# Gate tiles of a RG-LRU layer: neighbour rows stacked by ScalarE and VectorE instead of by transfers, for six of ten tiles

## The chip, the cores and the metric

One Trainium2 chip, one of its cores. The metric is the device time of one execution in microseconds (us). TensorE (PE) does the matrix products, ScalarE (ACT) and VectorE (DVE) the elementwise work, GpSimd (POOL) splits weights, SyncE (SP) issues the weight transfers. All arithmetic on the matrix side is fp32 accuracy from fp32r operands: a matrix or an activation is kept as a high part and the rest that the high part leaves (`hi`, `lo`), and a product is three matmuls, hi by hi, hi by lo and lo by hi.

## The reference, cut to what matters

A hybrid residual block on 1024 tokens of width 1024: a combined input projection, a Griffin recurrent branch of width 1280 next to sliding-window attention, a merge, an output projection, then SwiGLU. The change touches the two gates of the recurrent branch only:

```python
u = causal_depthwise_conv(u, conv_w) + conv_b            # width 1280
ub = u.reshape(B, S, 16, 80)                             # 16 blocks of 80 channels
r = sigmoid(einsum("bsnc,ncd->bsnd", ub, w_rg) + b_rg)   # block-diagonal
i = sigmoid(einsum("bsnc,ncd->bsnd", ub, w_ig) + b_ig)
log_a = -8 * r * softplus(-lru_lambda); a = exp(log_a)
b = sqrt(-expm1(2 * log_a)) * (i * u)
h = scan(h[t] = a[t] * h[t-1] + b[t]);  out = h * gelu(lru_gate)
```

The blocks have 80 channels and the tiles of the chip 128, so an output tile of 128 channels needs its own 128 channels of u and, at its edges, some channels of the tile before it or of the tile after it (up to 64).

## The kernel before, in words

The tokens are worked on in two halves of 512 (`h` = 0 and 1), so every matmul here has 512 columns. The 1280 channels are ten tiles, `j` = 0 to 9. For every tile, TensorE first computes the u projection (24 matmuls, `project`), and an iteration `j` of the loop `recurrent` on TensorE is: u projection of tile j, the gates of tile j-2 (`gates`), the gelu branch's projection of tile j (24 matmuls). The gates of tiles 8 and 9 come in `kvq`, each behind a projection of k.

ScalarE, in iteration j and strictly in this order: `conv_in` (copies of the projection and the first tap of tile j), `lru_out_hi` of tile j-3, `gate_fns` of tile j-2 (two tanh out of the gates' banks, exp, tanh; they wait for `gates(j-2)` of TensorE), `conv_hi` (the high part of the convolved tile j, called `uc_hi`, line 1383), `gate_root` (a table load and a square root, L1418), `mix` (DMA issues), `decay` (L1430, which waits for VectorE), `gelu` (L1424). VectorE does the other taps, the low part `uc_lo` (`conv_lo`, L1933, which waits for conv_hi), and the recurrence of tile j-2.

How neighbour rows reach a gate tile: matmuls contract over partitions, so rows of another tile have to lie on partitions of one operand.

- Tiles 1, 2, 3, 6, 7, 8 (`MIXED`) need rows of both neighbours. `mix` issues, once uc_lo of tile j exists, one DMA of 64 partitions (256 KB, both parts) from tile j into the operand `mix_hl` of tile j-1 and one into that of tile j+1, where these are MIXED. `mix_hl` has three slots (tile modulo 3). The gate then takes three matmuls of its own rows and three of the mixed operand, for each of the two gates: six a gate.
- Tiles 4, 5, 9 (`NEAR`) need 32 rows of one neighbour. Three DMAs of 64 KB stack the high part, the low part and the high part again on 96 partitions, and the weights are stacked to match (high, high, low), so one matmul (L927) takes the place of three: four a gate.
- Tile 0 needs rows of tile 1 only and reads tile 1's own operand: six a gate.

`gates` on TensorE waits, before its first matmul, for uc_lo of tile j+1 and for `mix_made`, the count of the DMAs of its slot. It also waits for its weights (`w_lo_made`): SyncE loads them (`load_gates`), GpSimd splits them (`split_gates`), four ring slots deep, a slot of weights being free again when TensorE has finished the block four before it (`blocks_done`).

Of the kernel before, what the change touches and what calls it, by code (L numbers as in the profile page):

```python
# [35 lines left out]
P = 128  # L36
# [33 lines left out]

MIXED = (1, 2, 3, 6, 7, 8)


NEAR = {4: (3, P - 32), 5: (6, 0), 9: (8, P - 32)}
STACK = ((0, 0), (32, 1), (64, 0))
STACKED = 96


def mix_count(h, j):
    same = range(j % 3, KR, 3)
    dmas = [2 if i in MIXED else len(STACK) if i in NEAR else 0 for i in same]
    return 16 * (h * sum(dmas) + sum(dmas[:j // 3 + 1]))

GATED = {"step": 0, "tail": 8}
A_STEP = [2, 2, 2, 2] + [3, 3, 2, 2]
# [100 lines left out]
def build(nc, x_d, par_d, alibi_d, eye_d, w_d, x1_d, out_d):  # L188
    with ExitStack() as ctx:
# [11 lines left out]
        def sem(name):  # L201
            return ctx.enter_context(nc.semaphore(name))
# [154 lines left out]
        def p1_raw(t):  # L357
# [39 lines left out]
        r_made, i_made, th_made, exp_made, root_made, a_made, gelu_made, lru_hi_made = (  # L397
            sem("r_made"), sem("i_made"), sem("th_made"), sem("exp_made"), sem("root_made"),
            sem("a_made"), sem("gelu_made"), sem("lru_hi_made"))
        iu_made, loss_made, amp_made, b_made, scanned, h_kept, lru_made, lru_lo_made = (  # L400
            sem("iu_made"), sem("loss_made"), sem("amp_made"), sem("b_made"), sem("scanned"),
            sem("h_kept"), sem("lru_made"), sem("lru_lo_made"))
# [101 lines left out]
        def a21_there(t):  # L504
            return (up_one_loaded[1], 16) if t == 1 else (up_loaded[1], 16 * single_loads(t))

        block = ctx.enter_context(nc.Block())


        @block.sync  # L510
        def _(sp_eng):
# [9 lines left out]
            def load_gates(dram, g, sizes, n, i0):  # L521

                off, i, half = 0, i0, slice(0, P // 2)
                for b, size in enumerate(sizes):
                    s = b % RING
                    wait_pos(sp_eng, w_lo_made, n + b - RING + 1)
                    if size == 4:
                        sp_eng.dma_start(w_raw[:, s, 0:CAP], dram[g, :, off:off + CAP])\
                            .then_inc(w_loaded[s], 16)
                    elif i in MIXED:  # L530
                        sp_eng.dma_start(w_raw[0:P // 2, s, P:2 * P],
                                         dram[g, 0:P // 2, off + 2 * P:off + 3 * P]).then_inc(mix_loaded[s], 16)
                        sp_eng.dma_start(w_raw[P // 2:P, s, P:2 * P],
                                         dram[g, P // 2:P, off:off + P]).then_inc(mix_loaded[s], 16)
                        sp_eng.dma_start(w_raw[:, s, 0:P], dram[g, :, off + P:off + 2 * P])\
                            .then_inc(w_loaded[s], 16)
                    elif i not in NEAR:
                        sp_eng.dma_start(w_raw[:, s, 0:2 * P], dram[g, :, off:off + 2 * P])\
                            .then_inc(w_loaded[s], 16)
                    else:  # L540
                        own = off + P
                        near, r = off if NEAR[i][0] < i else own + P, NEAR[i][1]
                        sp_eng.dma_start(w_raw[0:STACKED, s, P:2 * P],
                                         dram[g, r:r + 32, near:near + P]
                                         .rearrange("(o r) c -> o r c", o=1)
                                         .broadcast_to([len(STACK), 32, P])).then_inc(mix_loaded[s], 16)
                        sp_eng.dma_start(w_raw[:, s, 0:P], dram[g, :, own:own + P])\
                            .then_inc(w_loaded[s], 16)
                    off += size * P
                    i += size < 4 and sizes[b - 1] < 4  # L550
# [119 lines left out]
        def _(pool):  # L670
# [36 lines left out]
            def split_gates(sizes, n, i0):  # L707
                i = i0
                for b, size in enumerate(sizes):
                    s, w = b % RING, slice(0, (4 if size == 4 else 2) * P)  # L710
                    pool.wait_ge(w_loaded[s], (n // RING + b // RING + 1) * 16)
                    if size < 4 and i:
                        used[s] += 2 if i in MIXED else 1
                        pool.wait_ge(mix_loaded[s], 16 * used[s])
                    pool.wait_ge(blocks_done, n + b - RING + 1)
                    if size == 4 or i not in NEAR:
                        nc.gpsimd.tensor_scalar(w_hi[:, s, w], w_raw[:, s, w], 1.0, 0.0,  # L717
                                                ALU.mult, ALU.add).then_inc(w_hi_made, 1)
                    else:
                        nc.gpsimd.tensor_scalar(w_hi[:, s, 0:P], w_raw[:, s, 0:P], 1.0, 0.0,  # L720
                                                ALU.mult, ALU.add).then_inc(w_stacked, 1)
                        r, near = slice(0, STACKED), slice(P, 2 * P)
                        nc.gpsimd.tensor_scalar(w_hi[r, s, near], w_raw[r, s, near], 1.0, 0.0,
                                                ALU.mult, ALU.add).then_inc(w_hi_made, 1)
                        stacked.append(n)
                    if size < 4:
                        split_gate_lo(n + b, s, i)
                    else:
                        pool.wait_ge(w_hi_made, n + b + 1)
                        nc.gpsimd.tensor_tensor(w_lo[:, s, w], w_raw[:, s, w], rd(w_hi[:, s, w]),  # L730
                                                ALU.subtract).then_inc(w_lo_made, 1)
                    i += size < 4 and sizes[b - 1] < 4
# [111 lines left out]
        def _(pe):  # L844
# [58 lines left out]
            def gates(h, j, n, slot):  # L903

                J = j + KR * h
                pe.wait_ge(uc_lo_made, J + (1 if j == KR - 1 else 2))
                if j == KR - 1:
                    pe.wait_ge(r_made, J)
                    pe.wait_ge(i_made, J)
                if j:  # L910
                    pe.wait_ge(mix_made[j % 3], mix_count(h, j))
                own_hi, own_lo = uc_hi[:, j % 4, :], uc_lo[:, j % 4, :]
                for g in range(2):
                    s, out = (slot + g) % RING, ps[:, 4 + g, :]
                    pe.wait_ge(w_lo_made, n + g + 1)
                    own, near = slice(0, P), slice(P, 2 * P)
                    mm(out, w_hi[:, s, own], own_hi, start=True, stop=False)
                    mm(out, w_hi[:, s, own], own_lo, start=False, stop=False)
                    mm(out, w_lo[:, s, own], own_hi, start=False, stop=False)
                    if j not in NEAR:  # L920
                        near_hi, near_lo = ((mix_hi[:, j % 3, :], mix_lo[:, j % 3, :]) if j else
                                            (uc_hi[:, 1, :], uc_lo[:, 1, :]))
                        mm(out, w_hi[:, s, near], near_hi, start=False, stop=False)
                        mm(out, w_hi[:, s, near], near_lo, start=False, stop=False)
                        last = mm(out, w_lo[:, s, near], near_hi, start=False, stop=True)
                    else:
                        last = mm(out, w_hi[0:STACKED, s, near], mix_hi[0:STACKED, j % 3, :],  # L927
                                  start=False, stop=True)
                    last.then_inc(blocks_done, 1)
# [399 lines left out]
        def _(act):  # L1329
# [51 lines left out]
            def conv_hi(h, j, q):  # L1381
                act.wait_ge(taps, (j + KR * h) * 3 + 3)
                fn(uc_hi[:, q, :], uc_of(q), ACT.Copy).then_inc(uc_hi_made, 1)

            def mix(h, j):

                act.wait_ge(uc_lo_made, j + KR * h + 1)
                for to, r in ((j - 1, slice(0, P // 2)), (j + 1, slice(P // 2, P))):
                    if to in MIXED:
                        act.dma_start(rd(mix_hl[r, :, to % 3, :]), rd(uc_hl[r, :, j % 4, :]))\  # L1390
                            .then_inc(mix_made[to % 3], 16)
                    elif to in NEAR and NEAR[to][0] == j:
                        r = slice(NEAR[to][1], NEAR[to][1] + 32)
                        for row, part in STACK:
                            act.dma_start(rd(mix_hi[row:row + 32, to % 3, :]), rd(uc_hl[r, part, j % 4, :]))\
                                .then_inc(mix_made[to % 3], 16)

            def gate_fns(h, j, n):
                J = j + KR * h
# [477 lines left out]
        def _(dve):  # L1877
# [52 lines left out]
            def conv_lo(h, j, q):  # L1930
                J = j + KR * h
                dve.wait_ge(uc_hi_made, J + 1)
                tt(uc_lo[:, q, :], uc_of(q), rd(uc_hi[:, q, :]), ALU.subtract)\  # L1933
                    .then_inc(uc_lo_made, 1)

            def recurrence(h, j, q):
                J = j + KR * h
# [663 lines left out]
```

## Time and profile before

| | |
|---|---|
| time, median of 3 runs | 1620.09 us (1619.33 to 1626.31) |
| the profiled execution | 1621.06 us, of which the span is 1619.2 |
| granted TensorE clock, mean | 0.997 |
| TensorE busy | 1603.6 us, 99% of the span, 7390 matmuls |
| GpSimd, VectorE, ScalarE busy | 1234.4 (76%), 905.0 (56%), 572.3 us (35%) |
| chain that ended last | TensorE 90% |
| neighbour transfers | 24 of 256 KB (landing 4.7 us after issue, median), 18 of 64 KB (4.3 us) |

The first half's gates run from about 45 to 164 us of the span, the second half's from about 505 to 624 us. In the rows below, a gate tile begins on TensorE with its L917 (own high part); L925 is the last matmul of a MIXED gate. A bracket at the end of a row gives how long the engine had been idle before that instruction and what released it.

### The profile page before, as it was taken

What the parts mean: (1) busy time and instruction counts of PE and PEld (TensorE: products, weight loads), DVE (VectorE), ACT (ScalarE), POOL (GpSimd) and SP (SyncE); (2) the same over time, 40 slices, a digit from 0 to 9 for tenths busy, and PEclk for the clock granted to TensorE, in tenths of its full rate; (3) what the DMA queues carried; (4) which work ended last, traced back from release to release, by engine and by line L of the source; (5) the groups of instructions that cost most, each with busy time, mean ns of one, the idle gap of its engine ahead of it and who ended that gap; (6) DMA issues with size and microseconds to landing.
All of it is one profiled execution on the core that took longest, in us unless ns stands there. A gap on an engine that the chain in (4) does not pass through costs nothing.

```text
span 1619.2 us, 24286 instructions
## 1 busy us (share of the span) xinstructions
PE 1603.6 (99%) x7390; PEld 1327.0 (82%) x7390; DVE 905.0 (56%) x1158; ACT 572.3 (35%) x1078; POOL 1234.4 (76%) x1330
## 2 busy tenths in 40 slices
PE   9999999999999999999999999999999999999997
PEld 7888888888888888888888878888888888788887
DVE  6565646652165666676622579677865558405502
ACT  4787335532226885255422244100010013102100
POOL 5787866777777788777777777788887778877875
PEclk9999999999999999999999999999999999999999
DMA  5445432233344454522333583344422222733632
GB/s 165 131 120 131 132 91 80 74 101 93 97 144 128 121 133 114 166 77 74 92 97 95 150 286 107 97 118 117 119 75 75 65 65 69 245 93 114 222 107 87
DMA packets 121462, 188.86 MB, mean 117 GB/s; under 512 B 13668, under 2 KB 45796, under 8 KB 121380
## 3 DMA queue, kind: packets, MB, share of 16 engines
q1 hardware_dynamic: 97476, 144.03, 32.1%
q10 hardware_dynamic: 23904, 43.79, 8.2%
q8 instruction: 45, 0.74, 0.2%
q14 instruction: 37, 0.30, 0.1%
HBM read 162.73 MB, written 17.56 MB: 111 GB/s over the span
## 4 chain that ended last, share of the span: by engine, by line
PE 90%; DVE 4%; issue 2%; ACT 2%; ACTq 0%; DMA 0%; POOL 0%; DVEq 0%; SPq 0%; POOLq 0%
PE ps L872 14%; PE ps L871 14%; PE ps L870 14%; PE ps L1128 8%; PE ps L1127 8%; PE ps L1129 8%; PE ps L1225 4%; PE ps L1226 4%; PE ps L1227 4%; PE ps L950 1%; PE ps L946 1%; PE ps L947 1%; PE ps L1038 1%; DVE rows L2152 1%; DVE rows_r L2311 1%
## 5 line engine op out<-in xcount | busy, mean ns | idle before, releaser
L688 POOL TENSOR_TENSOR w_lo<-w_raw,w_hi 128x512 fp32r<-128x512 f32 (+2 forms) x374 | 448.3, 1199 | 31.2
L685 POOL TENSOR_SCALAR w_hi<-w_raw 128x512 fp32r<-128x512 f32 (+2 forms) x374 | 242.5, 648 | 194.4 <-PE ps L872 127.3
L872 PE MATMUL ps<-h_hi,w_lo 128*128 128x512 f32 x672 | 263.8, 393 | 0.0
L871 PE MATMUL ps<-h_lo,w_hi 128*128 128x512 f32 x672 | 263.6, 392 | 0.0
L870 PE MATMUL ps<-h_hi,w_hi 128*128 128x512 f32 x672 | 262.1, 390 | 0.7 <-DVE g_h L1950 0.6
L870 PEld LDWEIGHTS ps<-h_hi,w_hi 128*128 128x128 f32 x672 | 126.2, 188 | 28.9 <-DVE g_h L1950 1.5
L871 PEld LDWEIGHTS ps<-h_lo,w_hi 128*128 128x128 f32 x672 | 126.2, 188 | 27.5
L872 PEld LDWEIGHTS ps<-h_hi,w_lo 128*128 128x128 f32 x672 | 126.3, 188 | 26.1
L1127 PE MATMUL ps<-t,w_hi 128*128 128x512 f32 x352 | 138.2, 392 | 0.6 <-POOL w_lo L763 0.5
L1128 PE MATMUL ps<-t,w_hi 128*128 128x512 f32 x352 | 138.7, 394 | 0.0
L1129 PE MATMUL ps<-t,w_lo 128*128 128x512 f32 x352 | 136.6, 388 | 0.0
L1894 DVE TENSOR_TENSOR acc<-acc,sq 128x512 f32<-128x512 f32 x31 | 33.7, 1088 | 146.4 <-ACT sq L1620 134.2
L717 POOL TENSOR_SCALAR w_hi<-w_raw 128x512 fp32r<-128x512 f32 (+1 forms) x100 | 65.3, 653 | 45.5 <-PE ps L872 40.5
L730 POOL TENSOR_TENSOR w_lo<-w_raw,w_hi 128x512 fp32r<-128x512 f32 x72 | 93.8, 1303 | 6.0
L763 POOL TENSOR_TENSOR w_lo<-w_raw,w_hi 128x512 fp32r<-128x512 f32 x60 | 87.0, 1451 | 5.0
L1717 ACT ACTIVATE rstd_a<-rstd_a 128x512 f32<-128x512 f32 x22 | 13.9, 632 | 194.9 <-DVE rstd_a L2298 194.9
L1127 PEld LDWEIGHTS ps<-t,w_hi 128*128 128x128 f32 x352 | 66.1, 188 | 16.8 <-issue 1.4
L1129 PEld LDWEIGHTS ps<-t,w_lo 128*128 128x128 f32 x352 | 66.1, 188 | 14.8
L1128 PEld LDWEIGHTS ps<-t,w_hi 128*128 128x128 f32 x352 | 66.2, 188 | 13.1
L2119 DVE SCALAR_TENSOR_TENSOR tmp<-tmp,ps 128x512 f32<-128x512 f32 x16 | 11.0, 688 | 114.0 <-PE ps L872 114.0
L1620 ACT ACTIVATE sq<-ps 128x512 f32<-128x512 f32 (+1 forms) x15 | 9.0, 598 | 178.8 <-PE ps L1227 174.7
L1539 ACT ACTIVATE prob<-prob,stat 128x128 f32<-128x128 f32 x128 | 49.7, 389 | 63.3 <-DVE stat L2048 63.3
(389 smaller groups left out, 4105.7 us busy)
## 6 DMA issues: line engine op xcount, KB each, us to landing
w_raw<-w_f SPq DMA_DIRECT2D x68, 256.0 KB, 3.2
w_raw<-w_step SPq DMA_DIRECT2D x64, 256.0 KB, 2.8
w_raw<-w_b SPq DMA_DIRECT2D x64, 256.0 KB, 3.1
w_raw<-w_d SPq DMA_DIRECT2D x64, 256.0 KB, 2.7
w_raw<-w_a SPq DMA_DIRECT2D x96, 128.0 KB, 2.1
w_raw<-w_q SPq DMA_DIRECT2D x32, 256.0 KB, 3.1
w_raw<-w_o SPq DMA_DIRECT2D x32, 256.0 KB, 3.1
mix_hl<-uc_hl ACTq DMA_DIRECT2D x24, 256.0 KB, 4.7
```

Source lines behind the costliest of these rows:

```text
L685: nc.gpsimd.tensor_scalar(w_hi[:, s, w], w_raw[:, s, w], 1.0, 0.0, ALU.mult, ALU.add).then_inc(w_hi_made, 1)
L688: nc.gpsimd.tensor_tensor(w_lo[:, s, w], w_raw[:, s, w], rd(w_hi[:, s, w]), ALU.subtract).then_inc(w_lo_made, 1)
L717: nc.gpsimd.tensor_scalar(w_hi[:, s, w], w_raw[:, s, w], 1.0, 0.0, ALU.mult, ALU.add).then_inc(w_hi_made, 1)
L730: nc.gpsimd.tensor_tensor(w_lo[:, s, w], w_raw[:, s, w], rd(w_hi[:, s, w]), ALU.subtract).then_inc(w_lo_made, 1)
L763: nc.gpsimd.tensor_tensor(w_lo[:, s, :], src, rd(w_hi[:, s, :]), ALU.subtract)\
L870: mm(out, w_hi[:, s, w], x_hi, start=(k == 0), stop=False)
L871: mm(out, w_hi[:, s, w], x_lo, start=False, stop=False)
L872: last = mm(out, w_lo[:, s, w], x_hi, start=False, stop=(k == total - 1))
L1127: mm(ps[:, bank, :], w_hi[:, slot, w], x_hi[:, k, :], start=(q == 0), stop=False)
L1128: mm(ps[:, bank, :], w_hi[:, slot, w], x_lo[:, k, :], start=False, stop=False)
L1129: last = mm(ps[:, bank, :], w_lo[:, slot, w], x_hi[:, k, :], start=False, stop=(q == K2 - 1))
L1225: mm(out, w_hi[:, s, w], hi(k), start=(k == 0), stop=False)
```

## The change

Tiles 2 and 7 leave MIXED for a new group `BOTH`, and tile 0 joins NEAR. For these and for 4, 5 and 9 no DMA brings neighbour rows any more. Instead `conv_hi` of ScalarE, right after it has written the high part of tile j, copies 32 rows of it to each operand that needs them (each copy 32 partitions by 512), and `conv_lo` of VectorE, right after the low part, writes 32 rows of that (by the same subtraction):

- a NEAR tile: two copies on ScalarE (partitions 0 to 31 and 64 to 95), one on VectorE (32 to 63). One matmul for the neighbour, as before; tile 0 gets four matmuls a gate in place of six.
- a BOTH tile: from each neighbour 32 rows of the high part on ScalarE and 32 of the low part on VectorE, 128 partitions in all. The weights are loaded twice over to match, and two matmuls (high weights, low weights) take the place of three: five a gate in place of six.

By source tile, ScalarE gets three copies and VectorE two in each of j = 1 (for 2 and 0), 3 (for 2 and 4), 6 (for 7 and 5) and 8 (for 7 and 9), and none for the other j. `mix` is left with the transfers for tiles 1, 3, 6 and 8 (8 a half, of 21). SyncE issues five loads for a BOTH block in place of three, and two for a block of tile 0 in place of one; GpSimd splits a block of tile 0 in four instructions in place of two.

```diff
-MIXED = (1, 2, 3, 6, 7, 8)
-NEAR = {4: (3, P - 32), 5: (6, 0), 9: (8, P - 32)}
+MIXED = (1, 3, 6, 8)
+BOTH = (2, 7)
+NEAR = {0: (1, 0), 4: (3, P - 32), 5: (6, 0), 9: (8, P - 32)}
...
+        def near_of(j):
+            return [(to, slice(r, r + 32)) for to, (of, r) in NEAR.items() if of == j]
+        def both_of(j):
+            return ([(j + 1, slice(P - 32, P), 32)] if j + 1 in BOTH else
+                    [(j - 1, slice(0, 32), 0)] if j - 1 in BOTH else [])
...  # SyncE, load_gates
+                    elif i in BOTH:
+                        for row in range(0, P, 64):
+                            sp_eng.dma_start(w_raw[row:row + 32, s, P:2 * P],
+                                             dram[g, 0:32, off + 2 * P:off + 3 * P]).then_inc(mix_loaded[s], 16)
+                            sp_eng.dma_start(w_raw[row + 32:row + 64, s, P:2 * P],
+                                             dram[g, P - 32:P, off:off + P]).then_inc(mix_loaded[s], 16)
+                        sp_eng.dma_start(w_raw[:, s, 0:P], dram[g, :, off + P:off + 2 * P])\
                             .then_inc(w_loaded[s], 16)
...  # TensorE, gates
-                if j:
+                if j in MIXED:
                     pe.wait_ge(mix_made[j % 3], mix_count(h, j))
+                elif j in BOTH:
+                    pe.wait_ge(both_hi_made, both_count(h, j))
+                    pe.wait_ge(both_lo_made, both_count(h, j))
+                else:
+                    pe.wait_ge(near_hi_made, 2 * near_count(h, j))
+                    pe.wait_ge(near_lo_made, near_count(h, j))
...
+                    if j in BOTH:
+                        mm(out, w_hi[:, s, near], mix_hi[:, j % 3, :], start=False, stop=False)
+                        last = mm(out, w_lo[:, s, near], mix_hi[:, j % 3, :], start=False, stop=True)
...  # ScalarE
             def conv_hi(h, j, q):
                 act.wait_ge(taps, (j + KR * h) * 3 + 3)
                 fn(uc_hi[:, q, :], uc_of(q), ACT.Copy).then_inc(uc_hi_made, 1)
+                for to, r, row in both_of(j):
+                    act.wait_ge(uc_hi_made, j + KR * h + 1)
+                    fn(mix_hi[row:row + 32, to % 3, :], rd(uc_hi[r, q, :]), ACT.Copy)\
+                        .then_inc(both_hi_made, 1)
+                for to, r in near_of(j):
+                    act.wait_ge(uc_hi_made, j + KR * h + 1)
+                    for row in (0, 64):
+                        fn(mix_hi[row:row + 32, to % 3, :], rd(uc_hi[r, q, :]), ACT.Copy)\
+                            .then_inc(near_hi_made, 1)
...  # mix
-                    elif to in NEAR and NEAR[to][0] == j:
-                        r = slice(NEAR[to][1], NEAR[to][1] + 32)
-                        for row, part in STACK:
-                            act.dma_start(rd(mix_hi[row:row + 32, to % 3, :]), rd(uc_hl[r, part, j % 4, :]))\
-                                .then_inc(mix_made[to % 3], 16)
...  # VectorE, conv_lo, behind the subtraction that makes uc_lo
+                for to, r, row in both_of(j):
+                    tt(mix_hi[row + 64:row + 96, to % 3, :], uc_of(q)[r, :], rd(uc_hi[r, q, :]),
+                       ALU.subtract).then_inc(both_lo_made, 1)
+                for to, r in near_of(j):
+                    tt(mix_hi[32:64, to % 3, :], uc_of(q)[r, :], rd(uc_hi[r, q, :]), ALU.subtract)\
+                        .then_inc(near_lo_made, 1)
```

## Rows read from the trace of the kernel before

**Rows 1.** The page, busy us, share of the span, instructions.
```profile
PE 1603.6 (99%) x7390; PEld 1327.0 (82%) x7390; DVE 905.0 (56%) x1158; ACT 572.3 (35%) x1078; POOL 1234.4 (76%) x1330
```

**Rows 2.** The page, chain that ended last, shares of the span by engine.
```profile
PE 90%; DVE 4%; issue 2%; ACT 2%; ACTq 0%; DMA 0%; POOL 0%; DVEq 0%; SPq 0%; POOLq 0%
```

**Rows 3.** Timeline of PE: first matmul of gate tiles 1, 3, 6, 8, and 1 again.
```profile
58.87 0.39 PE L917 MATMUL ps<-uc_hl,w_hi 128*128 128x512 f32 x1
...
86.34 0.39 PE L917 MATMUL ps<-uc_hl,w_hi 128*128 128x512 f32 x1
...
125.97 0.47 PE L917 MATMUL ps<-uc_hl,w_hi 128*128 128x512 f32 x1
...
153.68 0.39 PE L917 MATMUL ps<-uc_hl,w_hi 128*128 128x512 f32 x1
...
518.73 0.39 PE L917 MATMUL ps<-uc_hl,w_hi 128*128 128x512 f32 x1
```

**Rows 4.** Waits, 28 to 182 us: who for whom, us, times, longest.
```profile
POOL w_hi L717 <- PE ps L872: 20.2, 22, 1.5
```

**Rows 5.** DMA issues at 80.98, 120.60, 148.32, 514.20: count, KB, us to landing.
```profile
mix_hl<-uc_hl ACTq DMA_DIRECT2D x1, 256.0 KB, 4.8
...
mix_hl<-uc_hl ACTq DMA_DIRECT2D x1, 256.0 KB, 5.3
...
mix_hl<-uc_hl ACTq DMA_DIRECT2D x1, 256.0 KB, 4.6
...
mix_hl<-uc_hl ACTq DMA_DIRECT2D x1, 256.0 KB, 3.7
```

**Rows 6.** Timeline of ACT, 65 to 82 us: iterations 3 and 4.
```profile
65.92 0.57 ACT L1383 ACTIVATE uc_hl<-ps 128x512 fp32r<-128x512 f32 x1
66.51 1.28 ACT L1418 ACT_TABLE_LOAD   x1
...
69.98 0.64 ACT L1430 ACTIVATE g_a<-g_r 128x512 f32<-128x512 f32 x1 [1.54 <-DVE g_s L1943]
...
72.91 0.20 ACT L1369 ACTIVATE u_raw<-u_carry 128x3 f32<-128x3 f32 x1 [0.39 <-PE ps L872]
...
75.64 0.69 ACT L1403 ACTIVATE g_r<-ps,half_b 128x512 f32<-128x512 f32 x1 [0.58 <-PE ps L925]
...
80.98 0.67 ACTq L1390 DMA_DIRECT2D mix_hl<-uc_hl  x1
```

**Rows 7.** Timeline of ACT, 113 to 121 us: iteration 7.
```profile
113.23 0.20 ACT L1369 ACTIVATE u_raw<-u_carry 128x3 f32<-128x3 f32 x1
...
114.76 0.62 ACT L1435 ACTIVATE lru_hi<-g_h 128x512 fp32r<-128x512 f32 x1
115.29 0.67 ACT L1403 ACTIVATE g_r<-ps,half_b 128x512 f32<-128x512 f32 x1
...
120.60 0.65 ACTq L1390 DMA_DIRECT2D mix_hl<-uc_hl  x1
```

**Rows 8.** Timeline of ACT, 140 to 149 us: iteration 9.
```profile
140.10 0.21 ACT L1369 ACTIVATE u_raw<-u_carry 128x3 f32<-128x3 f32 x1 [0.20 <-PE ps L872]
...
142.98 0.69 ACT L1403 ACTIVATE g_r<-ps,half_b 128x512 f32<-128x512 f32 x1 [0.73 <-PE ps L925]
...
148.32 0.71 ACTq L1390 DMA_DIRECT2D mix_hl<-uc_hl  x1
```

**Rows 9.** Timeline of ACT, 502 to 515 us: second half, iterations 1 and 2.
```profile
502.68 0.60 ACT L1424 ACTIVATE gy<-ps 128x512 f32<-128x512 f32 x1 [1.41 <-PE ps L872]
...
512.85 0.60 ACT L1383 ACTIVATE uc_hl<-ps 128x512 fp32r<-128x512 f32 x1 [0.86 <-DVE ps L1927]
...
514.20 0.60 ACTq L1390 DMA_DIRECT2D mix_hl<-uc_hl  x1
```

**Rows 10.** Timeline of ACT at 613 us: small copies.
```profile
613.16 0.30 ACT L1489 ACTIVATE k_hi<-k_hi 128x128 fp32r<-128x128 f32 x1
613.36 0.41 ACT L1490 ACTIVATE v_hl<-v_hl 64x256 fp32r<-64x256 f32 x1
```

More of the change, by code:

```diff
@@ L69, with both_count, near_count @@
 V_BLOCKS = [4, 4, 4, 4]
-MIXED = (1, 2, 3, 6, 7, 8)
-NEAR = {4: (3, P - 32), 5: (6, 0), 9: (8, P - 32)}
-STACK = ((0, 0), (32, 1), (64, 0))
+MIXED = (1, 3, 6, 8)
+BOTH = (2, 7)
+NEAR = {0: (1, 0), 4: (3, P - 32), 5: (6, 0), 9: (8, P - 32)}
+NEAR_LIST = list(NEAR)
 STACKED = 96
 def mix_count(h, j):
-    same = range(j % 3, KR, 3)
-    dmas = [2 if i in MIXED else len(STACK) if i in NEAR else 0 for i in same]
-    return 16 * (h * sum(dmas) + sum(dmas[:j // 3 + 1]))
+    same = [i for i in MIXED if i % 3 == j % 3]
+    return 32 * (h * len(same) + same.index(j) + 1)
+def both_count(h, j):
+    return 2 * (len(BOTH) * h + BOTH.index(j) + 1)
+def near_count(h, j):
+    return len(NEAR) * h + NEAR_LIST.index(j) + 1
 GATED = {"step": 0, "tail": 8}
@@ L399, in build @@
             sem("a_made"), sem("gelu_made"), sem("lru_hi_made"))
+        near_hi_made, near_lo_made = sem("near_hi_made"), sem("near_lo_made")
+        both_hi_made, both_lo_made = sem("both_hi_made"), sem("both_lo_made")
         iu_made, loss_made, amp_made, b_made, scanned, h_kept, lru_made, lru_lo_made = (
@@ L536, in load_gates @@
                             .then_inc(w_loaded[s], 16)
-                    elif i not in NEAR:
-                        sp_eng.dma_start(w_raw[:, s, 0:2 * P], dram[g, :, off:off + 2 * P])\
+                    elif i in BOTH:
[5 more added lines that the diff above has]
+                        sp_eng.dma_start(w_raw[:, s, 0:P], dram[g, :, off + P:off + 2 * P])\
                             .then_inc(w_loaded[s], 16)
                     else:
-                        own = off + P
+                        own = off + (P if i else 0)
                         near, r = off if NEAR[i][0] < i else own + P, NEAR[i][1]
@@ L545, in load_gates @@
                                          .rearrange("(o r) c -> o r c", o=1)
-                                         .broadcast_to([len(STACK), 32, P])).then_inc(mix_loaded[s], 16)
+                                         .broadcast_to([STACKED // 32, 32, P])).then_inc(mix_loaded[s], 16)
                         sp_eng.dma_start(w_raw[:, s, 0:P], dram[g, :, own:own + P])\
@@ L711, in split_gates @@
                     pool.wait_ge(w_loaded[s], (n // RING + b // RING + 1) * 16)
-                    if size < 4 and i:
-                        used[s] += 2 if i in MIXED else 1
+                    if size < 4:
+                        used[s] += 2 if i in MIXED else 4 if i in BOTH else 1
                         pool.wait_ge(mix_loaded[s], 16 * used[s])
@@ L919, in gates @@
                     mm(out, w_lo[:, s, own], own_hi, start=False, stop=False)
-                    if j not in NEAR:
-                        near_hi, near_lo = ((mix_hi[:, j % 3, :], mix_lo[:, j % 3, :]) if j else
-                                            (uc_hi[:, 1, :], uc_lo[:, 1, :]))
+                    if j in BOTH:
+                        mm(out, w_hi[:, s, near], mix_hi[:, j % 3, :], start=False, stop=False)
+                        last = mm(out, w_lo[:, s, near], mix_hi[:, j % 3, :], start=False, stop=True)
+                    elif j not in NEAR:
+                        near_hi, near_lo = mix_hi[:, j % 3, :], mix_lo[:, j % 3, :]
                         mm(out, w_hi[:, s, near], near_hi, start=False, stop=False)
```

## The prediction

> **What bounds the kernel now.** I read the page first, then the chain, then the timelines of the two stretches in which gates are computed. The page: TensorE is busy for 1603.6 of 1619.2 us [rows 1], and the chain that ended last lies on it for 90% [rows 2]. So a matmul that goes is worth its full pace, and a wait of TensorE costs its full length. The timeline of TensorE gives the pace: from the first matmul of gate tile 1 (58.87) to that of tile 3 (86.34) there are 120 (two gate tiles of 12, four projections of 24), 27.47 / 120 = 0.229 us each [rows 3]. (A row's own 0.39 is longer because matmuls overlap.)
>
> The second thing to see is how near TensorE is to waiting there. Between two gate tiles it has 48 projection matmuls, 11.0 us. In that time a closed chain runs: gates of tile j-2 end, ScalarE computes its four gate functions, then the high part of tile j, VectorE the low part, the transfer to tile j-1 is issued, lands, and TensorE may start the gates of j-1. Issue to landing is 4.8 us for the one issued at 80.98 [rows 5, 6], so it landed at 85.78, 0.56 ahead of the 86.34 at which tile 3 began. For tile 6 it was issued at 120.60 and took 5.3 [rows 5, 7]: 125.90, and tile 6 began at 125.97, its first matmul lasting 0.47 instead of 0.39 [rows 3], the mark of a short stall. For tile 8: 148.32 + 4.6 = 152.92 against 153.68 [rows 3, 5, 8]. So the margins are 0 to 0.8 us, and from landing to start it takes 0.07 (125.90 to 125.97).
>
> **What the change removes from TensorE.** Tile 0 loses two matmuls a gate, tiles 2 and 7 one each: (4 + 2 + 2) a half, 16 in all, 16 x 0.229 = 3.7 us. That is the gain if nothing else moved.
>
> **What it adds on ScalarE.** Three copies of 512 elements a partition behind the high part of tiles 1, 3, 6 and 8, ahead of the table load for the square root. The trace has no copy of 32 partitions by 512. Nearest rows: a copy of 128 x 128 lasts 0.30, one of 64 x 256 0.41 [rows 10]: twice the elements on half the partitions, and longer, so the partitions don't count. The high part itself, 128 x 512, lasts 0.57 [rows 6], and two instructions in a row of this length start 0.53 apart (114.76, 115.29) [rows 7]. Three, with a short wait for ScalarE's own write ahead of the first, make 1.7 us. Bounds: 3 x 0.20 = 0.6 by the shortest activation (128 x 3) and 3 x 0.69 = 2.1 by the longest of the high part's kind (L1403) [rows 6]. I take 1.7, the row nearest in length.
>
> The Trainium skill speaks against the change here: its page "ScalarE: Activation LUTs", section "What ACT_TABLE_LOAD costs", gives an activation with immediates as 186 ns and 0.833 ns for each element along the partition, with 93 ns of overlap between neighbours, so that cutting rows from 128 to 32 saves nothing. By it three copies are an estimated 1.65 us; the rows agree, 0.30 and 0.41 against 0.29 and 0.40. The sum would be the same to 0.05 us a place.
>
> **What this does to the chain.** The copies stand ahead of square root, decay, gelu and the next tile's `conv_in`, all in ScalarE's order; VectorE's recurrence waits for the square root, so decay (which waited 1.54 for VectorE [rows 6]) is late by the same 1.7. VectorE's own two additions (0.69 each by the form that it uses for the low part, an estimate) end before the later square root and are hidden by it. What I need is how much of 1.7 is left at the gate functions of the next iteration. Where ScalarE has no slack, `conv_in` to gate functions takes 113.23 to 115.29, 2.06 us [rows 7].
>
> - *Tile 1, first half.* The copies of iteration 1 stand ahead of a long wait for a projection; nothing is late. Tile 0's four matmuls are gained: -0.92.
> - *Tile 1, second half.* ScalarE's gelu of tile 1 had waited 1.41 for TensorE [rows 9], 0.3 less than the copies take; the inverse deviation and tile 2's taps on VectorE come behind it, and the high part of tile 2 waits for those taps (0.86), not for the gates. So the transfer leaves at 514.20 + 0.3, takes 3.7 [rows 5, 9], and tile 1 can start at 518.27, against 518.73 before [rows 3]: -0.46. Half of tile 0's gain meets the transfer.
> - *Tile 3, each half.* `conv_in` had waited 0.39 for TensorE, so it moves from 72.91 to 72.52 + 1.7 + 0.05 = 74.27, the gate functions to 76.33 in place of 75.64 [rows 6], 0.7 late. The transfer leaves at 81.68, lands at 86.48, tile 3 starts at 86.55, where TensorE would have been ready at 85.88 (0.46 earlier by tile 2's two matmuls). Against 86.34: +0.21, the gain of tile 2 spent and more.
> - *Tile 6, each half.* The worst place: the copies of iteration 6 come on a stretch where ScalarE waits for nothing, no bracket stands at 113.23 and 115.29 [rows 7], because gate tile 4 is short. The whole 1.7 reaches the transfer, and that was late already: +1.7.
> - *Tile 8, each half.* `conv_in` had waited 0.20, so the gate functions move from 142.98 [rows 8] to 139.90 + 1.7 + 0.05 + 2.06 = 143.71; the transfer leaves at 149.05 and lands at 153.65, start 153.72 against 153.68: +0.04. Tile 7's two matmuls are spent.
> - *Tiles 0, 2, 4, 5, 7, 9.* Their rows now come straight from ScalarE and VectorE: in iteration 3 the last copy ends at 65.92 + 0.59 + 1.7 = 68.2, over 4 us ahead of tile 2's gates. No wait. The issues of 26 transfers go from ScalarE's queue; they ran beside the square root and free nothing.
>
> Sum: first half -0.92 + 0.21 + 1.7 + 0.04 = +1.0; second half -0.46 + 0.21 + 1.7 + 0.04 = +1.5. Together 2.5 us slower.
>
> **What I cost at nothing.** SyncE's two more loads a block for tiles 2 and 7, and GpSimd's two more instructions for tile 0. In the first gate stretch GpSimd waits for TensorE to free a slot, 22 times, 20.2 us in all [rows 4], so weights are ahead of use. If that cover went, a late weight block would stop TensorE in the gate itself: below nothing is excluded, since no matmul waits for weights in this stretch, and above, I bound it by one such wait's longest, 1.5 us, for tiles 2 and 7 of each half: 6 us, unlikely.
>
> The profiled execution took 1621.06 us, 1.0 over the median of 1620.09; so 1623.6 by its own time, 1622.6 beside the median.
>
> **Rivals.**
> *The transfers land sooner.* 26 of 42 neighbour transfers go. For: the quickest of [rows 5] took 3.7. Against: the slow ones of 4.6 and 4.8 were alone at their issue. With 3.7 everywhere: tile 1 -0.92 and -0.46; tile 3 81.68 + 3.77 = 85.45, ready ahead of 85.88, -0.46; tile 6 122.30 + 3.77 = 126.07, +0.1; tile 8 152.82 ahead of 153.22, -0.46. Sum -1.7 and -1.3: 1617.1.
> The Trainium skill's page "DMA: Bandwidth & Descriptors", section "Anatomy of one DMA", fits a transfer as 2.0 us and its bytes at 436 GB/s, an estimated 2.6 us for 256 KB. By that no gate would ever wait, and the full 3.7 us would be gained, 1616.4; the rows say 3.7 to 5.3.
> *The copies are cheap*, 0.2 each, 0.6 together. Tile 3: gate functions at 72.52 + 0.6 + 0.05 + 2.06 = 75.23, transfer landed at 85.37, no wait, -0.46; tile 6 +0.6; tile 8 -0.46; tile 1 -0.92 and -0.76. Sum -1.2 and -1.1: 1617.8. Against it: [rows 10].
> *The transfers that stay land later.* SyncE puts four transfers of 32 rows beside the weights for each gate block of tiles 2 and 7, small pieces in the queues that the neighbour transfers share. If each lands 1 us later than in [rows 5], it is paid in full at tile 3, 6 and 8 in both halves and at tile 1 in the second, seven times: 2.5 + 7 = 9.5, 1629.6. From 0.8 us on it is a slowdown that can be told. For it: landings differ by 1.6 us within [rows 5]. Against: the bytes of neighbour transfers fall.
>
> **Chances.** Forecast 0.50, transfers sooner 0.20, cheap copies 0.15, transfers later 0.10, something else 0.05. A measurement of this kernel tells about 0.5%, 8.1 us, from no change: the first three cases all lie within it, of the fourth a good half lies above. So faster 0.02, same 0.92, slower 0.06. The range goes from 1616.2 (full gain) to 1627.0, which leaves out most of the fourth case; it also holds the 1.0 by which one execution differs from another.
>
> **What would show it.** Right: gate tiles 0, 2, 7 with 4 and 5 matmuls and no stall at their first; from the first matmul of tile 3 to that of tile 6 1.7 us more than before, with an idle TensorE ahead of tile 6; ScalarE's table load for the square root 1.7 later behind the high part in iterations 1, 3, 6 and 8. Wrong: copies under 0.4 us, landings for tile 6 under 4.5 us, or a TensorE wait that ends with GpSimd's low weights. A time under 1617 or over 1627 would mean that the chain is not the one I priced.

## The result, and the profile after

The changed kernel takes 1629.53 us (median of 16 runs, 1627.57 to 1635.71), the kernel before, timed beside it, 1620.72. The ratio is 1.0055, interval 1.0049 to 1.0062: 8.9 us slower, where 2.5 were forecast and the range ended at 1627.0. Some executions of most kernels here take 5 to 8 us more than their median, so medians and intervals are compared. The profiled execution has a span of 1627.2 us, 8.0 more than before, and that is what the intervals below have to explain.

The page and the chain of the changed kernel, the same two lines as [rows 1, 2]:

```profile
PE 1603.5 (99%) x7374; PEld 1323.9 (81%) x7374; DVE 928.7 (57%) x1174; ACT 585.8 (36%) x1102; POOL 1243.7 (76%) x1338
```

```profile
PE 82%; DVE 6%; ACT 6%; issue 4%; ACTq 1%; POOL 0%; DMA 0%; DVEq 0%; POOLq 0%
```

There are 16 matmuls fewer, as said, and TensorE is busy for as long as before. What moved is the chain: 90% of it lay on TensorE, now 82%, and ScalarE and VectorE have gained most of the rest. TensorE waits. The first lines of its waits over the whole changed kernel (us in all, times, longest) say for what; `L895` is the first matmul of a projection, `L948` the first of a gate tile, where the waits listed as issue ended with the neighbour transfer (that for tile 3 was issued at 81.68 and landed after 4.3 us, at 86.0; that for tile 6 at 123.18 and after 4.7, at 127.9):

```profile
PE ps L895 <- ACT gy L1461: 5.5, 6, 1.2
PE ps L948 <- issue: 2.7, 5, 0.7
```

The second is the wait that I had priced. The first, twice as long, I had not seen: the gelu branch's projection of tile j waits for gelu of tile j-1, which empties its bank.

The timeline of TensorE in the changed kernel, first matmul of gate tiles 1, 3, 6, 8 and of 1 again, as in [rows 3]:

```profile
57.53 0.47 PE L948 MATMUL ps<-uc_hl,w_hi 128*128 128x512 f32 x1
...
86.12 0.47 PE L948 MATMUL ps<-uc_hl,w_hi 128*128 128x512 f32 x1 [0.37 <-issue]
...
127.98 0.47 PE L948 MATMUL ps<-uc_hl,w_hi 128*128 128x512 f32 x1 [0.74 <-issue]
...
156.04 0.39 PE L948 MATMUL ps<-uc_hl,w_hi 128*128 128x512 f32 x1
...
521.80 0.47 PE L948 MATMUL ps<-uc_hl,w_hi 128*128 128x512 f32 x1 [0.32 <-issue]
```

Differences of such rows give the time of each stretch. First half / second half, us, from one profiled execution each; "no wait" is the number of matmuls in the changed kernel times 0.229:

| from gate tile to gate tile | 0 to 1 | 1 to 3 | 3 to 6 | 6 to 8 |
|---|---|---|---|---|
| before | 13.73 / 13.74 | 27.47 / 27.46 | 39.63 / 39.68 | 27.71 / 27.58 |
| forecast | 12.81 / 13.28 | 27.68 / 27.67 | 41.33 / 41.38 | 27.75 / 27.62 |
| changed | 12.87 / 13.34 | 28.59 / 29.58 | 41.86 / 41.87 | 28.06 / 28.06 |
| no wait | 12.8 | 27.0 | 39.4 | 27.0 |

The stretch 0 to 1 came out as forecast, and so did the sign of 3 to 6. The stretch 1 to 3 is where the working failed, by 0.9 and 1.9 us, then 3 to 6 by 0.5 and 6 to 8 by 0.3 to 0.4 each half. In sum the eight stretches are 7.2 us longer than before; the rest of the 8.0 lies outside them: 0.5 us less ahead of the first gate, 1.1 more between gate tile 9 of the first half and gate tile 0 of the second, 0.1 more behind the second half's gate tile 9.

What happens in one such iteration is seen on ScalarE of the changed kernel, iteration 3, the rows that answer to [rows 6]:

```profile
64.67 0.58 ACT L1416 ACTIVATE uc_hl<-ps 128x512 fp32r<-128x512 f32 x1
65.28 0.63 ACT L1419 ACTIVATE mix_hl<-uc_hl 32x512 fp32r<-32x512 f32 x1
65.93 1.28 ACT L1424 ACTIVATE mix_hl<-uc_hl 32x512 fp32r<-32x512 f32 x2
67.23 1.28 ACT L1455 ACT_TABLE_LOAD   x1
68.53 0.63 ACT L1455 ACTIVATE g_s<-g_r 128x512 f32<-128x512 f32 x1
71.88 0.63 ACT L1467 ACTIVATE g_a<-g_r 128x512 f32<-128x512 f32 x1 [2.72 <-DVE g_s L1986]
72.53 1.28 ACT L1461 ACT_TABLE_LOAD   x1
73.82 0.60 ACT L1461 ACTIVATE gy<-ps 128x512 f32<-128x512 f32 x1
74.32 0.20 ACT L1402 ACTIVATE u_raw<-u_carry 128x3 f32<-128x3 f32 x1
```

From the high part to the table load it is 67.23 - 64.67 = 2.56 us, before it was 0.59: the copies cost 1.97, not 1.7, because each takes 0.65 from start to start and they don't overlap. But from the square root to decay it is 3.35 us and the wait for VectorE 2.72, where before it was 1.54. ScalarE is late by 2.0, and decay by 3.1 (7.21 behind the high part in place of 4.06). On VectorE of the changed kernel, in the same stretch:

```profile
65.28 0.69 DVE L1970 TENSOR_TENSOR uc_hl<-ps,uc_hl 128x512 fp32r<-128x512 f32 x1 [2.89 <-ACT uc_hl L1416]
66.00 0.68 DVE L1973 TENSOR_TENSOR mix_hl<-ps,uc_hl 32x512 fp32r<-32x512 f32 x1
66.71 0.69 DVE L1976 TENSOR_TENSOR mix_hl<-ps,uc_hl 32x512 fp32r<-32x512 f32 x1
67.44 0.70 DVE L1982 SCALAR_TENSOR_TENSOR ps<-g_i,ps 128x512 f32<-128x512 f32 x1
69.27 0.82 DVE L1985 SCALAR_TENSOR_TENSOR g_r<-g_a,g_r 128x512 f32<-128x512 f32 x1 [1.13 <-ACT g_s L1455]
70.01 1.78 DVE L1986 SCALAR_TENSOR_TENSOR g_s<-g_a,g_s 128x512 f32<-128x512 f32 x1
```

and on GpSimd of the changed kernel:

```profile
68.93 0.62 POOL L742 TENSOR_SCALAR w_hi<-w_raw 128x512 fp32r<-128x512 f32 x1 [1.49 <-PE ps L897]
69.64 1.61 POOL L755 TENSOR_TENSOR w_lo<-w_raw,w_hi 128x512 fp32r<-128x512 f32 x1
```

The additions on VectorE are hidden, as forecast: they end at 67.40, 1.1 us before the square root starts. It is the update of g_s (L1986), two operands from SBUF, that takes 1.78 us in place of 0.68. It now falls on GpSimd's low-part split of a full weight block (69.64 to 71.25, itself 1.61 in place of 1.30). In the kernel before, the same split came 1.7 us behind the start of that update, and they missed each other:

```profile
69.17 0.68 DVE L1943 SCALAR_TENSOR_TENSOR g_s<-g_a,g_s 128x512 f32<-128x512 f32 x1
...
70.89 1.30 POOL L730 TENSOR_TENSOR w_lo<-w_raw,w_hi 128x512 fp32r<-128x512 f32 x1
```

Counted from the high part of tile 3 (65.92 before, 64.67 now), the split starts 4.97 us behind it in both kernels, and the update has moved from 3.25 to 5.34. So here ScalarE's delay has brought about the meeting of the two engines.

It is the same in five of the six iterations with copies in which a recurrence runs (3, 6 and 8 of both halves): an update of 1.78 to 1.79 us, and decay 2.9 to 3.2 us later behind the high part than before. The sixth is iteration 3 of the second half. Its own update takes 0.69 us, but in iteration 2, which has no copies, the update of tile 0 meets a split:

```profile
519.60 1.81 POOL L755 TENSOR_TENSOR w_lo<-w_raw,w_hi 128x512 fp32r<-128x512 f32 x1
...
520.17 1.79 DVE L1986 SCALAR_TENSOR_TENSOR g_s<-g_a,g_s 128x512 f32<-128x512 f32 x1
...
536.21 0.69 DVE L1986 SCALAR_TENSOR_TENSOR g_s<-g_a,g_s 128x512 f32<-128x512 f32 x1
```

Counted from gate tile 0's first matmul, that update starts 0.6 us later than before and the split 1.2 us earlier; the four matmuls that tile 0 has lost make 0.9 of this. Decay is 1.1 us late in iteration 2 and 1.8 in iteration 3, and the stretch 1 to 3 of that half pays for both. It is the largest miss in the table.

### The profile page after: what moved, and what is told of

Same layout as the page of the kernel before. It is cut to its first block, busy times and chain, and to the rows that moved or that the text cites. A ratio compares the mean times of both kernels' runs of the same rounds, so it can differ in the third digit from the quotient of the medians.

```text
span 1627.2 us, 24310 instructions
## 1 busy us (share of the span) xinstructions
PE 1603.5 (99%) x7374; PEld 1323.9 (81%) x7374; DVE 928.7 (57%) x1174; ACT 585.8 (36%) x1102; POOL 1243.7 (76%) x1338
## 4 chain that ended last, share of the span: by engine, by line
PE 82%; DVE 6%; ACT 6%; issue 4%; ACTq 1%; POOL 0%; DMA 0%; DVEq 0%; POOLq 0%
PE ps L896 12%; PE ps L897 12%; PE ps L895 12%; PE ps L1160 8%; PE ps L1162 8%; PE ps L1161 8%; PE ps L1258 4%; PE ps L1259 4%; PE ps L1260 4%; PE ps L983 1%; PE ps L1071 1%; PE ps L979 1%; PE ps L980 1%; ACT L1455 1%; DVE g_s L1986 1%
## 5 line engine op out<-in xcount | busy, mean ns | idle before, releaser
L895 PE MATMUL ps<-h_hi,w_hi 128*128 128x512 f32 x672 | 263.6, 392 | 6.6 <-ACT gy L1461 5.5
L895 PEld LDWEIGHTS ps<-h_hi,w_hi 128*128 128x128 f32 x672 | 126.3, 188 | 37.4 <-ACT gy L1461 8.4
L755 POOL TENSOR_TENSOR w_lo<-w_raw,w_hi 128x512 fp32r<-128x512 f32 x72 | 100.6, 1397 | 6.0
L742 POOL TENSOR_SCALAR w_hi<-w_raw 128x512 fp32r<-128x512 f32 (+1 forms) x96 | 61.1, 636 | 40.7 <-PE ps L897 38.7
L788 POOL TENSOR_TENSOR w_lo<-w_raw,w_hi 128x512 fp32r<-128x512 f32 x60 | 87.0, 1450 | 5.0
```

The costliest lines, as they stand in the source:

```text
L788: nc.gpsimd.tensor_tensor(w_lo[:, s, :], src, rd(w_hi[:, s, :]), ALU.subtract)\
L895: mm(out, w_hi[:, s, w], x_hi, start=(k == 0), stop=False)
```

## The experiments

Theory A, read from the traces above: ScalarE's copies ahead of the square root make the recurrence late, the late update of g_s meets GpSimd's split and becomes later still, and TensorE pays through gelu and through the transfers. Rival B: SyncE's and GpSimd's added work on the weights. Rival C: VectorE's added low parts. Every ratio is against the kernel before on the same chip.

**e1: the copies later.**

```diff
                 fn(uc_hi[:, q, :], uc_of(q), ACT.Copy).then_inc(uc_hi_made, 1)
+
+            def stack_hi(h, j, q):                 # the same copies, out of conv_hi
                 for to, r, row in both_of(j):
...
                     conv_hi(h, j, j % 4)
                     gate_root(h, j - 2)
+                    stack_hi(h, j, j % 4)
                     mix(h, j)
```

> The changed kernel with ScalarE's stacking copies moved from ahead of the square root to behind it (iterations 2 to 9; VectorE's part stays where it is). Theory A (ScalarE's order: three copies of 0.65 us ahead of the square root make the recurrence, gelu and the next transfer late, and push VectorE's second update of g_s into GpSimd's low-part split, 1.78 in place of 0.68 us): the copies fall into the 1.5 us that ScalarE waits for VectorE there, decay is late by 0.5 to 0.9 us only, that update falls back under 1.1 us, TensorE's waits for gelu (5.5 us) go; about 1618.5 us, 1617 to 1622. Rival B (weights: SyncE's extra loads, GpSimd's extra instructions for tiles 0, 2, 7): nothing moves, 1629 us. Rival C (VectorE's two added low parts delay the recurrence): little moves, 1627 to 1629 us.

Measured 1622.46 us, ratio 1.0012 (1.0002 to 1.0022). One move in ScalarE's order gives back some 7 of the 9 us, with every load, split and low part of the change in place: rival B is out as the cause of these. The stretches: 12.85 / 13.49, 27.06 / 29.27, 40.88 / 40.00, 27.09 / 27.10. Four are within 0.15 us of "no wait". The second of 1 to 3 is the furthest from it, and the profile has a wait of 0.96 for gelu there; one iteration ahead of it, tile 0's update (516.70) still takes 1.78 us. The time is a little above the range expected (1617 to 1622), so something was left.

**e2: VectorE's low parts later too.**

```diff
...  # with the edit of e1
                 stt(g_s[:], g_a[:], 1.0, g_s[:], ALU.add, ALU.mult).then_inc(amp_made, 1)
+                if stack:
+                    stack_lo(h, stack, stack % 4)  # the low parts, out of conv_lo
```

> As the run before it, and VectorE's low parts moved too, behind the update of g_s. Theory A: VectorE's chain up to decay is as in the kernel before, decay late by what is left of the copies, about 0.4 us; 1617.5 us, at most 1 us below the run with ScalarE's copies alone. Rival B: 1629 us. Rival C: the drop comes here and not with ScalarE's copies alone, to about 1618 us.

Measured 1622.75 us, ratio 1.0012 (1.0002 to 1.0021): no different from e1, and 5 us over what A had for it. Nothing for rival C; but the low parts, moved back, now hold up two gate tiles themselves (TensorE's first matmul there waits for them, 1.25 and 0.64 us).

**e3: the copies alone, on the kernel before.**

```diff
+        spare = at("spare", [P, T], F32R, reg_v + 7 * 4 * KV_HEADS * 2 * HD)
...
                 fn(uc_hi[:, q, :], uc_of(q), ACT.Copy).then_inc(uc_hi_made, 1)
+                if j in (1, 3, 6, 8):
+                    act.wait_ge(uc_hi_made, j + KR * h + 1)
+                    for row in (0, 32, 64):
+                        fn(spare[row:row + 32, :], rd(uc_hi[0:32, q, :]), ACT.Copy)
```

> The kernel before with three idle copies of 32 x 512 on ScalarE behind the high part of tiles 1, 3, 6 and 8, into memory that nobody reads; all transfers, matmuls and loads stay. Theory A: the copies alone cost as much as the change or more, since the transfers for tiles 2 and 7 are still issued behind the square root, 2 us late: 10 to 16 us slower, 1631 to 1637 us. Rivals B and C: no change, 1620 to 1622 us.

Measured 1629.77 us, ratio 1.0063 (1.0042 to 1.0084), a little under the range expected. The copies by themselves, with no other part of the change, make the kernel 9.1 us slower. This is not quite the whole of what the change adds: it is 8.9 us slower although it has 16 matmuls, 3.7 us, fewer. How much of that gain is swallowed where TensorE waits anyhow, e3 does not tell. VectorE of this kernel shows the same second step in iteration 3:

```profile
70.11 0.87 DVE L1947 SCALAR_TENSOR_TENSOR g_r<-g_a,g_r 128x512 f32<-128x512 f32 x1 [2.66 <-ACT g_s L1423]
70.90 1.78 DVE L1948 SCALAR_TENSOR_TENSOR g_s<-g_a,g_s 128x512 f32<-128x512 f32 x1
```

No low part is added on VectorE here, and the update is still 1.78 us long.

**e4: gelu ahead of decay.**

```diff
-                    decay(h, j - 2)
                     gelu(h, j, n + 6, j % 4)
+                    decay(h, j - 2)
```

> The changed kernel with one swap in ScalarE's order: gelu of tile j ahead of decay of tile j-2, so gelu no longer waits behind VectorE's recurrence. Copies, VectorE's part, loads and splits all stay. Theory A: the door through which the delay reaches TensorE is gelu and what stands behind it; gelu fills the wait for VectorE, TensorE's waits for gelu go, the next gate functions wait for TensorE again and the transfers of tiles 3, 6, 8 leave in time: about 1618 us, 1617 to 1621. Rival B: 1629 us. Rival C: between, 1624 to 1629, since VectorE is as late as before.

Measured 1625.96 us, ratio 1.0031 (1.0018 to 1.0043): 3.6 us below the change, a third of the fall that A expected, and inside the range given for rival C, which this run leaves open; e6 settles it. TensorE's waits for gelu are gone, those at the gates rise from 2.7 to 5.4 us. So gelu was one door and not the only one. ScalarE of this kernel, iteration 7, shows the other:

```profile
115.90 0.63 ACT L1472 ACTIVATE lru_hi<-g_h 128x512 fp32r<-128x512 f32 x1 [0.83 <-DVE g_h L2000]
116.44 0.67 ACT L1440 ACTIVATE g_r<-ps,half_b 128x512 f32<-128x512 f32 x1
```

`lru_out_hi` waits for VectorE's recurrence and stands ahead of the gate functions, so a late recurrence makes the next gates late whatever gelu does.

**e5: the square root in PSUM.**

```diff
+        def gs_of(j):
+            return ps[:, 5, :] if j < 8 else g_s[:]
...  # ScalarE
-                fn(g_s[:], g_r[:], ACT.Sqrt).then_inc(root_made, 1)
+                fn(gs_of(j), g_r[:], ACT.Sqrt).then_inc(root_made, 1)
...  # VectorE
-                stt(g_s[:], g_a[:], 1.0, g_s[:], ALU.add, ALU.mult).then_inc(amp_made, 1)
+                stt(g_s[:], g_a[:], 1.0, gs_of(j), ALU.add, ALU.mult).then_inc(amp_made, 1)
...  # TensorE, gates
+                    if g and J:
+                        pe.wait_ge(amp_made, KR * h + min(j, 8))
```

> The changed kernel with the square root written to a PSUM bank that is free at that time (the second gate's), so VectorE's update of g_s reads one operand from SBUF and one from PSUM instead of two from SBUF; TensorE's second gate waits for that update of the tile before. Copies keep their place ahead of the square root. Theory A with a second part (the late update meets GpSimd's low-part split, which lengthens it): the update takes 0.7 us in all iterations in place of 1.78 in those with copies, decay and gelu come 1.1 us earlier there, TensorE's six waits for gelu (5.5 us) shrink to under 1.5 us; about 1625 us, 1623 to 1627. If the length of the update has nothing to do with its operands: 1.78 stays, 1629 us.

Measured 1622.47 us (the kernel before beside it: 1621.03), ratio 1.0001 (0.9988 to 1.0015): lower than A expected, with the copies where the change has put them. All executions of that line, of the changed kernel first, then of e5 (duration ns min/median/max):

```profile
L1986 DVE SCALAR_TENSOR_TENSOR g_s<-g_a,g_s x20: 678/1101/1793, 54.1 to 645.9; 128x512 f32<-128x512 f32 x20
```

```profile
L1991 DVE SCALAR_TENSOR_TENSOR g_s<-g_a,ps x16: 673/680/682, 54.6 to 614.2; 128x512 f32<-128x512 f32 x16
L1991 DVE SCALAR_TENSOR_TENSOR g_s<-g_a,g_s x4: 1777/1783/1784, 163.9 to 640.4; 128x512 f32<-128x512 f32 x4
```

With one operand in PSUM it is 0.68 us in all 16 cases, in six of which GpSimd's split of a full block was running when the update started; the four that were left with both operands in SBUF are 1.78 in all four. TensorE's waits for gelu fall from 5.5 to 0.9 us; those at the gates, with the copies still ahead of the transfers in ScalarE's order, rise from 2.7 to 4.3. So the lengthened update is shown to be the larger part of the loss: some 7 of the 9 us by the medians, 4.6 of 8.0 in the profiled executions (that of e5 took 1624.44 us, 2 more than its median).

The stretches of e5 are 12.85 / 13.36, 27.41 / 28.97, 41.14 / 41.51, 27.42 / 27.71: seven of the eight within 0.35 us of the row "forecast" above. The eighth, 1 to 3 of the second half, is 1.3 longer. There VectorE's update ahead of this one, which still has both operands in SBUF, meets a split:

```profile
530.89 1.29 POOL L758 TENSOR_TENSOR w_lo<-w_raw,w_hi 128x512 fp32r<-128x512 f32 x1
...
530.97 1.76 DVE L1990 SCALAR_TENSOR_TENSOR g_r<-g_a,g_r 128x512 f32<-128x512 f32 x1 [1.10 <-ACT ps L1460]
```

**e6: VectorE's low parts alone, on the kernel before.**

```diff
+        spare = at("spare", [P, T], F32R, reg_v + 7 * 4 * KV_HEADS * 2 * HD)
...
                     .then_inc(uc_lo_made, 1)
+                if j in (1, 3, 6, 8):
+                    for row in (0, 32):
+                        tt(spare[row:row + 32, :], uc_of(q)[0:32, :], rd(uc_hi[0:32, q, :]), ALU.subtract)
```

> The kernel before with VectorE's two additions alone: two idle 32 x 512 subtractions behind the low part of tiles 1, 3, 6 and 8, into memory that nobody reads. Theory A: they end before or shortly after the square root; at most 0.7 us late into the recurrence, 1620 to 1622.5 us. Rival C (VectorE's share is what costs): most of the 9 us, 1626 to 1630.

Measured 1621.51 us, ratio 1.0013 (0.9997 to 1.0029): no effect that can be told, and the interval ends below the 1626 at which rival C began. Rival C is out.

**e7: tiles 2 and 7 alone.** One copy and one low part an iteration; 4, 5, 9 by transfers, 0 unstacked.

```diff
-MIXED = (1, 2, 3, 6, 7, 8)
+MIXED = (1, 3, 6, 8)
+BOTH = (2, 7)
 NEAR = {4: (3, P - 32), 5: (6, 0), 9: (8, P - 32)}
...  # for BOTH: loads, waits, matmuls, copies and low parts as in the change
```

> Half of the change: tiles 2 and 7 stacked by ScalarE and VectorE (one copy and one low part in each of iterations 1, 3, 6, 8, in place of three and two), tiles 4, 5, 9 by transfers and tile 0 unstacked as before. Eight matmuls fewer, 1.8 us. Theory A: 0.65 us ahead of the square root is nearly covered by ScalarE's 0.4 to 0.6 us of slack at tiles 3 and 8 and paid at tile 6 only (0.7 each half); no wait for gelu; 1619 to 1621 us. If the cost were in the loads and weights of tiles 2 and 7 (rival B), all of it would be here: 1627 to 1629.

Measured 1620.55 us, ratio 0.9991 (0.9977 to 1.0006). The five loads a block of tiles 2 and 7 are all here, and cost nothing: rival B once more. With a third of the copies the loss is gone; eight matmuls fewer are not enough to be told from none.

**e8 and e10: the copies later and the square root in PSUM.** Both edits of e1 and e5 together, the same kernel timed twice.

> ScalarE's copies behind the square root (as in the run with the copies later) and the square root in PSUM. Theory A: the two causes are taken away together; left are the late start at tile 6, where ScalarE has no slack (about 0.5 us each half), and the transfers; 1618 to 1620 us, 2 to 4 us below the run with the copies later alone.

> The version with the copies behind the square root and the square root in PSUM, timed closer: 1617.5 to 1619.5 us, the interval clear of 1.

Measured 1618.99 us, ratio 0.9988 (0.9975 to 1.0001), and 1617.86 us, 0.9986 (0.9975 to 0.9997). It is the one version that came out faster than the kernel before (the first interval just reaches 1, the second does not), by 2.2 us of the 3.7 that 16 matmuls are worth, and some 11 below the change. Its stretches in the second run: 12.84 / 13.31, 27.01 / 27.14, 39.84 / 40.14, 27.10 / 27.10. What is left of the waits at its gates:

```profile
PE ps L953 <- issue: 0.8, 2, 0.5
```

**e9: the square root in PSUM alone, on the kernel before.** The edit of e5.

> Control: the kernel before, with the square root in PSUM alone. There the update of g_s already takes 0.68 us in most iterations of the loop (0.95 in four), so theory A expects next to nothing, 1619.5 to 1621 us. If the gain of the later runs came from this edit by itself and not from the change, it would show here as 2 us or more.

Measured 1620.65 us, ratio 1.0008 (0.9995 to 1.002): nothing, as expected. The gain of e8 and e10 is that of the change, once its two costs are taken away.

**e11: e10 with gelu ahead of decay.** The edit of e4.

> The same with gelu ahead of decay. Theory A: gelu comes earlier but decay, behind gelu and its table load, 1.5 us later, so the scan and the next lru_out_hi, which stands ahead of the gate functions in ScalarE's order, are late; the transfers at tiles 3 and 6 pay; no gain over the version without the swap, 1618 to 1622 us. If gelu is the only door that matters, 1616.5 to 1618.

Measured 1621.13 us, ratio 1.0001 (0.9989 to 1.0012): 3.3 us worse than e10, as A expected. TensorE's waits at the gates are 2.8 us. The other door took over: in iteration 7 `lru_out_hi` waits 0.80 us for VectorE, where in e10 it waits for nothing, and the gate functions start behind it. That fits e4; what each part of it costs here was not taken apart.

## Why the prediction was wrong, step by step

- *What bounds the kernel, and the pace of 0.229 us.* Right. "No wait" by that pace is met within 0.15 us in five of the eight stretches of e10.
- *Removed from TensorE: 3.7 us.* Right in size; 2.2 of it can be had.
- *Three copies, 1.7 us.* Mis-sized: 1.97. The spacing of 0.53 was taken from two instructions of [rows 7] that overlap; the copies of 32 rows start 0.65 apart. The estimate of 1.65 by the Trainium skill's page "ScalarE: Activation LUTs", section "What ACT_TABLE_LOAD costs", was low in the main for the same reason, the overlap that it states.
- *"Decay is late by the same 1.7."* This is the step that failed. I moved VectorE's recurrence along with ScalarE as if its instructions kept their lengths. The update of g_s went from 0.68 to 1.78 us in five of six iterations with copies, so decay was 2.9 to 3.2 us late there and not 1.7; e5 shows what this second part is worth, some 7 of the 9 us by the medians. With it gone, decay is 1.7 to 2.1 us late in the same five iterations and seven of eight stretches are near the forecast.
- *"What I need is how much of 1.7 is left at the gate functions."* Failed too: it names one door. The second is the wait of a projection for gelu of the tile before; I had not set the two times beside each other. In the changed kernel it opened six times, 5.5 us. In e5 it stayed shut in the five with decay 1.7 to 2.1 us late and opened in the sixth, iteration 3 of the second half, with 2.9.
- *Tile 1.* Right in both halves (12.87 and 13.34 against 12.81 and 13.28). In the second, half of tile 0's gain meets the transfer, as named, but the size is partly luck: the transfer left 0.6 us late and not 0.3, and landed after 3.4 us and not 3.7.
- *Tiles 3 and 8.* Off by 0.9 to 1.9 and 0.3 to 0.4 us, by the two steps above (for tile 3 of the second half, by tile 0's update one iteration earlier); *tile 6* by 0.5. There the copies were on a stretch with no slack, as said. That the miss is no larger is luck: counted from gate tile 3, the transfer left 2.8 us late and not 1.7, and landed after 4.7 us in place of 5.3. With one copy (e7) the stretch is 40.26 and 39.78 against 39.63 and 39.68.
- *The rival of sooner landings* had a part of the truth: the transfer for tile 3 landed after 4.3 us in place of 4.8, those for tile 6 after 4.7 in place of 5.3, that for tile 8 after 3.2 in place of 4.6. It was given back with the rest. The rival of cheap copies and that of later landings were wrong; that the latter's 1629.6 is the time measured is luck. The fit of 2.6 us from the Trainium skill's page "DMA: Bandwidth & Descriptors", section "Anatomy of one DMA", is given there for transfers that GpSimd issues; these are ScalarE's, and those of the changed kernel landed after 3.2 to 5.8 us.
- *Cost at nothing: weights and VectorE's additions.* Right: e7, e1 and e6. But GpSimd's split, which costs TensorE no wait, came in by another way, through VectorE.
- *What would show it.* From tile 3 to tile 6 it is 2.2 us more, not 1.7, with TensorE idle for 0.74 ahead of tile 6, and the table load 1.97 us later behind the high part. Of the signs of being wrong only the time over 1627 came, and it meant what it was said to mean: the chain was not the one priced.

The collision could have been read from the trace of before: of the 20 executions of that update, those of gate tiles 8 and 9, at 163.47 and 176.99 us in the first half and at 623.24 and 636.76 in the second, took 1.78 us there too. All executions in the kernel before (duration ns min/median/max), and the one at 163.47 beside the split that it met:

```profile
L1943 DVE SCALAR_TENSOR_TENSOR g_s<-g_a,g_s x20: 677/680/1784, 55.8 to 636.8; 128x512 f32<-128x512 f32 x20
```

```profile
162.97 1.73 POOL L688 TENSOR_TENSOR w_lo<-w_raw,w_hi 128x512 fp32r<-128x512 f32 x1
...
163.47 1.78 DVE L1943 SCALAR_TENSOR_TENSOR g_s<-g_a,g_s 128x512 f32<-128x512 f32 x1
```

The rows of iteration 3 of the changed kernel read as operations that take turns: the split starts at 69.64 while VectorE's L1985 is running to 70.09, ends 1.16 behind that, and the update of g_s ends 0.54 behind the split, each 0.14 less than its length alone (1.30 and 0.68). The Trainium skill states a cause that fits in its page "SBUF — State Buffer", section "SBUF: two separate sides": VectorE and GpSimd share a pair of ports, and a VectorE operation with two SBUF inputs and a GpSimd operation that reads SBUF exclude each other, the first to start holding the pair. e5 agrees: with one of the two inputs in PSUM the update keeps its 0.68.

## What to carry to other kernels

An instruction put ahead of others on an engine that works strictly in order is not a constant added to them: follow every engine that it makes late, and ask on what each late instruction then falls. Read the spread of a line's durations, not its mean, before moving it in time; here, two lengths for one shape meant a neighbour. And of a late producer list all who wait for it, with their slack, before choosing the one that is paid.

## What the runs showed that was not expected

- An update of 128 x 512 with both inputs in SBUF takes 0.68 us alone and 1.78 us beside GpSimd's split of a weight block, which stretches from 1.30 to 1.6 us and more itself (up to 1.81). Beside a smaller operation of GpSimd it takes a length between: 1.10 us beside the first pass over a block (its high part, L742, itself 0.99 in place of 0.62), 0.95 beside the split of a 128 x 128 one. With one input in PSUM it takes 0.68 us in 16 of 16 cases.
- Copies of 32 rows by 512 on ScalarE take 0.63 us and follow each other at 0.65, without the overlap that the two full-height instructions of [rows 7] show (0.53).
- Between gate tile 9 of the first half and gate tile 0 of the second the changed kernel takes 344.18 us in place of 343.07. With the square root in PSUM (e5, e8) it is 343.08 and 343.07 again. Half of the 1.1 us lies ahead of the first projection of q, which waits for the recurrence of tile 9 (0.92 us of idle TensorE in place of 0.12); the other half is one matmul of the attention, at 252.34, which waits 0.36 us for VectorE. Why that one waits was not traced.
